# A streaming encoder step on one core: 240 dummy TensorE products put between the warm-up and the first real product

## The reference, cut to what matters

```python
h = h + 0.5 * swiglu(rmsnorm(h, ln_ffn1[i]), w1_gate[i], w1_up[i], w1_down[i])
u = rmsnorm(h, ln_mix[i])
mix = mamba2_mixer(u, ...) if i < N_A else latent_attention(u, ...)
h = h + mix
h = h + 0.5 * swiglu(rmsnorm(h, ln_ffn2[i]), w2_gate[i], w2_up[i], w2_down[i])
h = h + (p[i] @ w_ple_in[i]) * sigmoid(rmsnorm(h, ln_ple[i]) @ w_ple_gate[i])
```

## Time and profile before

| | |
|---|---|
| two executions that were timed | 1845.85 us and 4646.25 us; their median is given as 3246.05 us |
| the profiled execution | 1845.71 us, its span from first to last instruction 1843.9 us |
| PE busy / PEld busy | 1813.3 us (98%) / 1733.8 us (94%) |
| DVE / ACT / POOL busy | 1134.6 us (62%) / 828.0 us (45%) / 228.2 us (12%) |
| mean granted TensorE clock | 0.998 of full |

### The profile page before, as it was taken

How to read it: one execution, slowest core, us unless ns; L and a number is a source line. 1 busy time by engine, 2 the same in 40 slices (tenths; PEclk the granted TensorE clock), 3 DMA queues, 4 the chain that set the end, 5 groups by cost and what they waited for, 6 DMA issues and landing times.

```text
span 1843.9 us, 28269 instructions
## 1 busy us (share of the span) xinstructions
PE 1813.3 (98%) x10561; PEld 1733.8 (94%) x10561; DVE 1134.6 (62%) x1709; ACT 828.0 (45%) x1424; POOL 228.2 (12%) x278
## 2 busy tenths in 40 slices
PE   9999999999999999999999999999998999999998
PEld 8999999899888999999999999986777999999998
DVE  6545447879889645544775454456778856454445
ACT  5333235665564433333553333346666544333333
POOL 1000011311311000011400001123111131000110
PEclk9999999999999999999999999999999999999999
DMA  6444444556452544444343444441124533434442
GB/s 211 122 129 125 141 139 154 156 206 232 123 205 86 193 124 128 123 148 137 115 147 119 131 124 139 137 165 40 47 71 141 179 115 123 136 117 134 141 137 77
DMA packets 68292, 249.74 MB, mean 135 GB/s; under 512 B 8312, under 2 KB 10616, under 8 KB 66928
## 3 DMA queue, kind: packets, MB, share of 16 engines
q1 hardware_dynamic: 58736, 206.89, 36.4%
q0 software_dynamic: 9472, 41.70, 6.7%
HBM read 235.77 MB, written 12.12 MB: 134 GB/s over the span
## 4 chain that ended last, share of the span: by engine, by line
PE 83%; DVE 10%; ACT 3%; DMA 2%; issue 2%; POOL 1%; SPq 0%; DVEq 0%; ACTq 0%; POOLq 0%
PE pair L1900 23%; PE pair L1902 23%; PE pair L1901 23%; DVE wlo L1240 2%; PE pair L2401 2%; PE pair L2310 2%; PE pair L2311 2%; PE pair L2312 2%; DVE cy L1368 1%; DVE S L1464 1%; DMA wv<-in_wv 1%; DMA raw<-in_stream 1%; PE pair L1907 0%; PE pair L1909 0%; PE pair L1908 0%
## 5 line engine op out<-in xcount | busy, mean ns | idle before, releaser
L1900 PE MATMUL pair<-xh,whi 128*128 128x384 f32 x1928 | 649.7, 337 | 3.5 <-DVE xl L1250 3.0
L1902 PE MATMUL pair<-xh,wlo 128*128 128x384 f32 x1928 | 644.5, 334 | 0.0
L1901 PE MATMUL pair<-xl,whi 128*128 128x384 f32 x1928 | 644.3, 334 | 0.0
L1240 DVE TENSOR_TENSOR wlo<-raw,whi 128x1024 fp32r<-128x1024 f32 (+3 forms) x372 | 464.8, 1251 | 176.9 <-ACT whi L703 168.4
L703 ACT ACTIVATE whi<-raw 128x1024 fp32r<-128x1024 f32 (+2 forms) x369 | 378.3, 1029 | 273.6 <-PE pair L1902 258.8
L1900 PEld LDWEIGHTS pair<-xh,whi 128*128 128x128 f32 x1928 | 361.9, 188 | 10.3 <-issue 4.7
L1901 PEld LDWEIGHTS pair<-xl,whi 128*128 128x128 f32 x1928 | 362.0, 188 | 1.6 <-issue 1.0
L1902 PEld LDWEIGHTS pair<-xh,wlo 128*128 128x128 f32 x1928 | 361.9, 188 | 0.0
L1260 DVE TENSOR_TENSOR tg<-pair,rstd 128x384 f32<-128x384 f32 x88 | 49.0, 557 | 328.2 <-PE pair L1902 327.5
L1900 PE MATMUL pair<-ah,whi 128*128 128x384 f32 x704 | 236.6, 336 | 0.0
L1902 PE MATMUL pair<-ah,wlo 128*128 128x384 f32 x704 | 236.6, 336 | 0.0
(11 more groups left out here) (400 smaller groups left out, 2243.6 us busy)
## 6 DMA issues: line engine op xcount, KB each, us to landing
raw<-in_stream SPq DMA_DIRECT2D x372, 512.0 KB, 3.6
S<-in_ssm POOLq DMA_DIRECT2D x4, 2048.0 KB, 9.1
out_ssm_s<-S POOLq DMA_DIRECT2D x4, 2048.0 KB, 7.8
seg<-acs_rows POOLq DMA_DIRECT2D x12, 512.0 KB, 6.4
cTb<-in_cacheT POOLq DMA_DIRECT2D x10, 512.0 KB, 4.1
kn<-rs_rows SPq DMA_DIRECT2D x16, 264.0 KB
lowC<-in_cache SPq DMA_DIRECT2D x8, 512.0 KB, 3.2
lowA<-in_cacheT POOLq DMA_DIRECT2D x6, 512.0 KB, 5.3
```

What stands on the lines that cost most here:

```text
L1240: V.tensor_tensor(wlo[:, r, 0:w], raw[:, r, 0:w], whi[:, r, 0:w].bitcast(F32), ALU.subtract).then_inc(lo_ready, 1)
L1900: M(out, whi[:, r, ws], mh_(k), start=first and k == k0, stop=False)
L1901: M(out, whi[:, r, ws], ml_(k), start=False, stop=False)
L1902: ins = M(out, wlo[:, r, ws], mh_(k), start=False, stop=last and k == k1 - 1)
```

## The change

POOL sets three slices of `ah` and one of `al` to 1.0 at the start, between `ones` and `xp`. PE, behind the warm-up loop and before `gate_up(0, 0)`, waits for both and issues 240 matmuls of float32r operands with 384 columns each. Five times it waits for its own last matmul (semaphore `tried`). In order:

- 24 into one bank (6), then 24 into banks 0 and 1 in turn
- 48 with 64 rows, on the lower and the upper half in turn, banks 2 and 3
- 48 with 32 rows, on the four quarters in turn, banks 0 to 3
- 16 each: 96 rows; 64 output partitions; moving operand shifted by 16 elements; by 32; taken as two pieces of 192; shifted by 8

```diff
             pool.memset(ones[:, :], 1.0).then_inc(filled, 1)
+            pool.memset(ah[:, 0:3, :].bitcast(F32), 1.0).then_inc(warm_in, 1)
+            pool.memset(al[:, 0:1, :].bitcast(F32), 1.0).then_inc(warm_in, 1)
             pool.memset(xp[:, :, :], 0.0).then_inc(filled, 1)
...
             for _ in range(WARM):
                 M(bank[6][:, 0:P], ones[:, :], ones[:, :], start=True, stop=True)
+            pe.wait_ge(warm_in, 2)
+            for _ in range(24):
+                ins = M(bank[6][:, 0:TOK], al[:, 0, 0:P], ah[:, 0, :], start=True, stop=True)
+            ins.then_inc(tried, 1)
+            pe.wait_ge(tried, 1)
+            for i in range(24):
+                ins = M(bank[i % 2][:, 0:TOK], al[:, 0, 0:P], ah[:, 0, :], start=True, stop=True)
+            ins.then_inc(tried, 1)
+            pe.wait_ge(tried, 2)
+            for i in range(48):
+                at = slice(64 * (i % 2), 64 * (i % 2) + 64)
+                ins = M(bank[2 + i % 2][:, 0:TOK], al[at, 0, 0:P], ah[at, 0, :], start=True, stop=True)
+            ins.then_inc(tried, 1)
+            pe.wait_ge(tried, 3)
+            for i in range(48):
+                at = slice(32 * (i % 4), 32 * (i % 4) + 32)
+                ins = M(bank[i % 4][:, 0:TOK], al[at, 0, 0:P], ah[at, 0, :], start=True, stop=True)
+            ins.then_inc(tried, 1)
+            pe.wait_ge(tried, 4)
+            for i in range(16):
+                ins = M(bank[5][:, 0:TOK], al[0:96, 0, 0:P], ah[0:96, 0, :], start=True, stop=True)
+            for i in range(16):
+                ins = M(bank[6][0:64, 0:TOK], al[:, 0, 0:64], ah[:, 0, :], start=True, stop=True)
+            for i in range(16):
+                ins = M(bank[4][:, 0:TOK], al[:, 0, 0:P], ah[:, 0:2, :].rearrange("p a t -> p (a t)")[:, 16:16 + TOK], start=True, stop=True)
...
+            for i in range(16):
+                ins = M(bank[6][:, 0:TOK].rearrange("p (a t) -> p a t", a=2), al[:, 0, 0:P], ah[:, 0:2, 0:192], start=True, stop=True)
...
+            ins.then_inc(tried, 1)
+            pe.wait_ge(tried, 5)
             gate_up(0, 0)
```

More of the change, by code:

```diff
@@ L256, in build @@
         filled = sem("filled")
+        warm_in = sem("warm_in")
         h_new = sem("h_new")
@@ L393, in build @@
         y_st = sem("y_st")
+        tried = sem("tried")
         mask_ld = sem("mask_ld")
@@ L1989, in _ @@
                 M(bank[6][:, 0:P], ones[:, :], ones[:, :], start=True, stop=True)
+            pe.wait_ge(warm_in, 2)
[24 more added lines that the diff above has]
+            for i in range(16):
+                ins = M(bank[5][:, 0:TOK], al[:, 0, 0:P], ah[:, 0:2, :].rearrange("p a t -> p (a t)")[:, 32:32 + TOK], start=True, stop=True)
+            for i in range(16):
+                ins = M(bank[6][:, 0:TOK].rearrange("p (a t) -> p a t", a=2), al[:, 0, 0:P], ah[:, 0:2, 0:192], start=True, stop=True)
+            for i in range(16):
+                ins = M(bank[4][:, 0:TOK], al[:, 0, 0:P], ah[:, 0:2, :].rearrange("p a t -> p (a t)")[:, 8:8 + TOK], start=True, stop=True)
+            ins.then_inc(tried, 1)
+            pe.wait_ge(tried, 5)
             gate_up(0, 0)
```

## The result

The changed kernel took 1875.79 and 1877.30 us, median 1876.55. Against the 1845.85 us of the kernel before that is a ratio of 1.0155, interval 1.0137 to 1.0173. The changed kernel is 1.6% slower; the forecast was 1875. (The other time of before, 4646.25 us, moves its median to 3246.05 but says nothing of this change: in 49 further executions of the kernel before it did not come back, as 48 took 1846.1 to 1853.5 us and one 1992.8 with a mean granted clock of 0.85, and what made it is not known.)

The account below looks back on a forecast made before the run. PE, busy 1813.3 of 1843.9 us, was taken as the bound. Dummies of 33.4 us put the first real product 31.0 us later; less 1.75 us returned, 1845.71 + 29.25 = 1875 us, range 1872 to 1886.

Parts of the forecast that it names:

- first dummy: Start of the added products on PE behind the warm-up: next start possible at 7.57 us, after POOL's fills are done.
- last 96, two changes, one wait: Final dummies on PE: 16.6 us at 0.1733 each, 0.5 for entering and leaving 64 output columns, 0.33 for the wait.
- The rest of the trace should be the old one, moved.: Everything behind the first product of `down` keeps its old course, only 29.25 us later.
- what bounds the kernel: PE, busy 1813.3 of 1843.9 us: work put before its first real product moves all that follows, unless PE idled there.
- parts of the array overlap, and by how much: Dummies on row halves run in pairs, 4.2 us; those on row quarters in fours, 2.1 us.
- what comes back: Two later idle places of PE, for block 1's split and the norm's sum, vanish: 1.75 us together.
- two changes of the array's division: Into and out of the 64 output columns without a wait: 0.5 us together, bounds nothing and 1 us.
- The waits: PE's five waits for its own last matmul among the dummies: 0.33 us each, 1.65 us together, bounds 0.8 and 3.
- Rival A: Halves and quarters of float32r don't overlap: 16.6 us instead of 6.3, total 1885.3 us; chance 0.16, including equal-sized other losses.
- a falling clock: Warning sign, no size given: a clock that fell during the quarters would make the sum wrong upwards.
- B: Only part overlaps: halves in sequence 1879 us, quarters in sequence 1881, quarters held up by issuing 1877; chance 0.17.
- C: PE's 480 added instructions come late: one or two pauses add 1.5 to 3 us, 1877 to 1878; counted within the 0.65.

Follow-up runs that it names:

- second trace: The unaltered changed kernel measured once more beside the kernel before, on one chip: 1881.39 us, ratio 1.0170.
- the kernel that makes it come true: Changed kernel with the row halves in blocks of 24 and the quarters in blocks of 12 instead of in turn: 1894.66 us, ratio 1.0246.

## Where the forecast held, and the step that failed

The forecast was 29.25 us slower, 1.6%, and 30.7 were measured (25.3 to 31.9): a slowdown well clear of the measurement's own uncertainty, and below the 2% that I had called no change. In the profiled execution the shift is 30.0 us: 29.4 of them stand at the first product of `down`, where 29.25 were forecast, and 0.6 to 0.7 come behind it. The steps, each with its value in the changed kernel's trace:

| step | forecast | changed kernel |
|---|---|---|
| first dummy | 7.57 us | 7.99 |
| 48 whole-array, two waits | 8.3 + 0.66 = 9.0 | 8.99 |
| 48 halves, one wait | 4.2 + 0.33 = 4.5 | 4.53 |
| 48 quarters, one wait | 2.1 + 0.33 = 2.4 | 2.45 |
| last 96, two changes, one wait | 16.6 + 0.5 + 0.33 = 17.5 | 17.04 |
| first real product | 41.0 | 41.00 |
| first product of `down` | 224.7 | 224.82 |
| span | 1873.15 | 1873.9 |

**The step that failed: "The rest of the trace should be the old one, moved."** All that lies behind the start of `down` was put at nothing. From there to the end before takes 1843.9 - 195.45 = 1648.4 us, the changed kernel 1649.1, and in its second trace 1651.8: 0.7 and 3.4 us more. The runs don't show this as a price of the dummies, though a share of it can't be excluded. The kernel with the fills alone and no dummy takes 1650.3, and the 14 traces lie between 1648.4 and 1653.8: that of before is the lowest, and that with 192 quarter products, one of the longest at the start, is level with it (1887.9 - 239.46). The forecast was built on one execution of 1845.71 us, and 48 later ones took 1846.1 or more. Why the part differs from one execution to the next stays open; what it is made of can be seen in the stretch behind 1207 us, below.

**Right up to `down`: what bounds the kernel.** A microsecond of PE's time at the start is a microsecond there, but for the idle places. The run with 12 dummies and the one with 48 show both sides of that.

**Right: parts of the array overlap, and by how much.** This was read off float32 rows and holds for float32r with 64 and 32 rows. It was shown by taking the overlap away (8.0 instead of 4.5 us for the halves, at full clock; the quarters' 11.7 instead of 2.4 hold the fall of the clock as well) and by stretching it to 240 products. By the Trainium skill's factor of 3.07 (TensorE: Matmul & The Clock Gate, "Measured speedup vs the span model"; given for 512 columns) the quarters would have taken 2.7 us, an estimate. Measured are 12 x 0.173, the full factor of 4, and the measurement decides.

**Right: what comes back.** 185.5 - 183.8 = 1.7 us, seen in both the changed kernel (224.82 - 41.00 = 183.8) and the one with 48 dummies.

**Two terms were off, in opposite directions.** The warm-up ended later than in before (8.23 instead of 7.73 us), so the first dummy came 0.42 us late. And the two changes of the array's division at the 64 output columns, 0.5 us in my sum, cost nothing. I had taken them from line 2099, where the type of the operands changes too. The two misses, +0.42 and -0.42 us, cancel: that the first real product stands at 41.00 to the hundredth is luck.

**The waits: right in sum, wrong in part.** 0.33 us each was right as the distance goes, but taking all five out gave back 1.04, not 1.65 us, as three of them hid a pause of the array's own.

**Behind 1207 us PE is not the bound.** In the profiled execution the shift is 29.45 us up to there and 30.0 at the end. It doesn't grow steadily: 29.75 at 1219 us of the old time, 28.2 at 1230, 29.9 at 1337, 29.5 at 1412, 30.0 from 1500 on. The first fall is the clock. In before it stood at 0.50 from 1224 to 1227 us, in the changed kernel it did not fall, and PE does ten matmuls more in the same 10 us. First before, then after:

```profile
1220.00:1230.00 10.00, 7.88 (x38) 0.83 0.19 54
```

```profile
1249.40:1259.40 10.00, 7.88 (x48) 1.00 0.19 56
```

What the clock gave comes back as waits for other engines. At 1332.89 us of the old time PE had no wait; the changed kernel waits there for ACT's `kn`, and a little in two places behind it. A second low stretch of the clock in before, 0.50 from 1408.5 to 1411.4 us, has its counterpart in a shorter wait for DVE's `Pb` there. One line of after, then before and after:

```profile
1362.01 0.51 PE L2347 MATMUL pair<-wkh,cTh 128*128 128x512 f32 x1 [0.80 <-ACT kn L1083]
```

```profile
1412.03 0.36 PE L2385 MATMUL pair<-cTh,whi 128*128 128x264 f32 x1 [0.66 <-DVE Pb L1842]
```

```profile
1441.52 0.36 PE L2422 MATMUL pair<-cTh,whi 128*128 128x264 f32 x1 [1.73 <-DVE Pb L1846]
```

So here a faster PE waits longer, and what ends the waits is work of ACT and DVE. The 0.6 us are what is left of gains and losses of 1 to 2 us each, and no run separates them. The second measurement's interval (28.8 to 34.0 us) holds both 29.3 and 30.0, and single executions of one kernel differ by up to 8 us.

**Rival A had the wrong price.** It was put at 39.6 us, and the kernel that makes it come true took 45.6 (1894.66 - 1849.05); in its trace 44.4 stand at the first product of `down` (239.87 - 195.45). Not the lost overlap was mis-sized, but the clock was left out, although I had named a falling clock as what could make the sum wrong. Its verdict, slower by over 2%, was right with either number. B's price for the quarters alone in sequence (1881 us, 35 above before) was short for the same reason: 38.1 us were measured. C did not happen: the 480 instructions came in time.

## What to carry to other kernels

Where an engine is the bound, the cost of more work is its own time less the idle time that it fills, and both can be read to a few tenths from the distances between starts. An end-to-end forecast can't be as fine as that: the part that the change doesn't touch moved by up to 5 us from trace to trace. Products that use a part of the rows took a part of the time here when their neighbours in program order used other rows and other banks, and the full time when they shared both; put them in turn, not in blocks. What a run of small products takes from the clock is paid by the large ones behind it, so read the granted clock of the stretch that follows as well.

## What the hardware did that I had not expected

A busy PE can lose its clock. With 48 products on one row quarter at a time PE was busy for the whole stretch, and the granted clock fell from 1.00 to 0.50 within 1 to 5 us of their start. It came back some 6 us after the 96-row products behind them had begun, which cost these 2.4 us in either run. With one half at a time or two quarters at a time for 16 us it did not fall.

The warm-up's 40 matmuls took between 6.1 and 7.5 us in the traces: 19 of their distances in before and 24 in the changed kernel were some 0.213 us, the others 0.111. So the start of everything behind it moves by over 1 us from one execution to the next, while the 33.0 us of the dummies were the same to 0.01 in the two traces of the changed kernel.
